# Two largest sorted experts ahead of the four small ones, and the later down weights on ScalarE's DMA queue

## The reference, cut to what matters

```python
DEPTH = 2, SEQ = 512, D_MODEL = 1024, N_EXPERTS = 16, N_GROUPS = 4, TOP_K = 2, D_FF_EXPERT = 256

def reference(...):
    for i in range(DEPTH):
        y = gated_deltanet(x) if i == 0 else latent_attention(x)
        x = layernorm(ALPHA * x + y)
        y = grouped_moe(x, router_w, router_bias, w_gate[i], w_up[i], w_down[i])
        x = layernorm(ALPHA * x + y)

def grouped_moe(x, ...):           # x: 512 tokens
    scores = sigmoid(x @ router_w)
    # one group of four experts is selected per token, and the top two experts in it
    gates = ...                    # (512, 16), two entries per row are not zero
    hid = silu(einsum('td,edf->tef', x, w_gate)) * einsum('td,edf->tef', x, w_up)
    return einsum('tef,efd->td', hid * gates[..., None], w_down)
```

## Time and profile before

| | |
|---|---|
| time, median of 3 runs | 1362.57 us (1362.47 to 1367.99) |
| time of the profiled execution | 1367.03 us |
| its span in the trace | 1365.2 us |
| TensorE busy | 1295.4 us, 95% of the span |
| VectorE, ScalarE, GpSimd busy | 58%, 25%, 22% |
| experts of layer 0, pass 0's first expert matmul to the last pass's end | 734.7 to 881.4 us |
| experts of layer 1, the same | 1182.3 to 1328.9 us |

### The profile page before, as it was taken

How to read it: one execution, slowest core, us unless ns; L and a number is a source line. 1 busy time by engine, 2 the same in 40 slices (tenths; PEclk the granted TensorE clock), 3 DMA queues, 4 the chain that set the end, 5 groups by cost and what they waited for, 6 DMA issues and landing times. The chain is left out here.

```text
span 1365.2 us, 22220 instructions
## 1 busy us (share of the span) xinstructions
PE 1295.4 (95%) x7858; PEld 744.5 (55%) x7858; DVE 791.5 (58%) x1751; ACT 346.4 (25%) x773; POOL 303.2 (22%) x536
## 2 busy tenths in 40 slices
PE   8999999999999999999998998999999998899895
PEld 5467575766758667487754332355454454533232
DVE  2867777676676757675676441294253546644227
ACT  3322322222222222223221221122422322122110
POOL 2264434052340613406022000220000000200025
PEclk9999999999999999999999998999999999899898
DMA  6440505225052250533337999730211138499962
GB/s 213 133 111 19 158 7 164 65 73 157 6 165 65 75 153 13 151 130 89 144 123 282 365 412 411 264 116 1 89 45 38 34 109 319 185 349 411 412 247 107
DMA packets 172631, 218.84 MB, mean 160 GB/s; under 512 B 57297, under 2 KB 107857, under 8 KB 172561
## 3 DMA queue, kind: packets, MB, share of 16 engines
q1 hardware_dynamic: 134736, 167.10, 35.8%
q10 hardware_dynamic: 32736, 32.77, 7.2%
q0 software_dynamic: 5088, 18.02, 3.6%
HBM read 184.58 MB, written 33.29 MB: 160 GB/s over the span
## 5 line engine op out<-in xcount | busy, mean ns | idle before, releaser
L531 PE MATMUL bank<-xT,wgu 128*128 128x512 f32 x448 | 196.2, 593 | 3.0 <-DVE wgu L1236 2.8
L2106 PE MATMUL bank<-wgu,moe_xgT 128*32 128x512 f32 x1120 | 158.8, 606 | 2.9 <-ACT moe_xgT L2224 2.9
L531 PEld LDWEIGHTS bank<-xT,wgu 128*128 128x128 f32 x448 | 83.6, 190 | 100.3 <-issue 100.1
L1236 DVE SCALAR_TENSOR_TENSOR wgu<-bank,taps,wgu 128x510 f32<-128x510 f32 (+1 forms) x128 | 95.6, 748 | 62.6 <-ACT wgu L833 56.7
L617 PE MATMUL bank<-wd,xT 128*128 128x256 f32 x512 | 118.9, 383 | 0.3 <-DVE res L1329 0.3
L583 PE MATMUL bank<-wd,oT 128*128 128x512 f32 x224 | 105.3, 593 | 0.0
L617 PEld LDWEIGHTS bank<-wd,xT 128*128 128x128 f32 x512 | 94.5, 190 | 16.2 <-issue 3.3
L2141 PE MATMUL bank<-wd,moe_hidT 128*32 128x512 f32 x704 | 84.8, 625 | 12.4 <-issue 11.2
L2106 PEld LDWEIGHTS bank<-wgu,moe_xgT 128*32 128x32 f32 x1120 | 43.8, 112 | 73.5 <-issue 65.9
L2406 DVE TENSOR_TENSOR moe_hid<-moe_silu,bank 128x256 f32<-128x256 f32 x22 | 9.3, 421 | 113.0 <-ACT moe_silu L2230 113.0
L2106 PE MATMUL bank<-moe_fifth,moe_xgT 128*32 128x512 f32 x288 | 70.6, 594 | 0.0
(11 more groups left out here) (374 smaller groups left out, 2320.3 us busy)
## 6 DMA issues: line engine op xcount, KB each, us to landing
wd<-moe_w_down SPq DMA_DIRECT2D x32, 1024.0 KB, 13.0
wgu<-moe_w_gate SPq DMA_DIRECT2D x26, 1024.0 KB, 10.5
wgu<-moe_w_up SPq DMA_DIRECT2D x26, 1024.0 KB, 13.4
wgu<-dn_w_in SPq DMA_DIRECT2D x32, 512.0 KB, 4.5
slots_x<-gains SPq DMA_DIRECT2D x5, 1920.0 KB, 10.2
wgu<-gate_rows SPq DMA_DIRECT2D x14, 512.0 KB, 5.3
wd<-dn_w_out ACTq DMA_DIRECT2D x14, 512.0 KB, 4.2
wd<-dn_w_in ACTq DMA_DIRECT2D x7, 1024.0 KB, 5.2
```

The costliest lines, as they stand in the source:

```text
L531: mm = pe.matmul(bank[:], wqkv[:, ct, k], xT[:, k], start=k == 0, stop=k == KD - 1)
L1236: ins = nc.vector.scalar_tensor_tensor(out=conv[:, ct, lo:hi], in0=bank[:, lo + d:hi + d], scalar=w[:, j:j + 1], in1=conv[:, ct, lo:hi], o ...
L2106: mm = pe.matmul(ps[2][seats].rearrange("p (a f) -> p a f", a=2), xgT[:, j % ROW_BUFS, k, seats], gate_up_of(e)[:, :, k], start=k == 0, st ...
```

## The change

It moves the position of the four small experts from v = 5 to 8 to v = 7 to 10 (`FIRST_SMALL` = 7), and puts the two largest sorted experts at v = 5 and 6; the rest keep their order (smallest to larger, the third largest last). With that, which passes a position takes part in is:

| position | 5 | 6 | 7 | 8 | 9 | 10 | 11 to 15 |
|---|---|---|---|---|---|---|---|
| passes before | 3, 4 | 4 | 4, 5 | 5 | 5, 6 | 6, 7 | as after |
| passes after | 3, 4 | 4, 5 | 5 | 5, 6 | 6 | 6, 7 | as before |

So pass 4 needs positions 5, 6, 7 before and 5, 6 after; pass 5 needs 7, 8, 9 before and 6, 7, 8 after; pass 6 needs 9, 10 before and 8, 9, 10 after. What frees a buffer moves too: gate and up 11 wait for pass 5 (before: 4), 13 for pass 6 (before: 5), down 10 for pass 5 (before: 4), down 12 for pass 6 (before: 5); the others keep theirs.

The down matrices of positions 4 to 15 are no longer started by SP but by ScalarE (`next_downs(j)`, behind `results(j)` and ahead of `store(j)`), which reads `order` for each itself. SP starts the gate and up pairs alone, in order of position. The router computes the new places with two more small operations ahead of `place` and one fewer behind it.

```diff
-FIXED, SMALL = 5, 4
+FIXED, SMALL, FIRST_SMALL = 5, 4, 7
-TILES = [v for v in range(NE) for _ in range(2 if FIXED <= v < FIXED + SMALL else 3)]
+TILES = [v for v in range(NE) for _ in range(2 if FIRST_SMALL <= v < FIRST_SMALL + SMALL else 3)]
...
+FIRST_SORTED = TILES.index(FIRST_SMALL) + 3 * (SORTED - 1) - (SORTED - 1)
+WRAP = len(TILES) - TILES.index(FIXED)
...
-            def load_gate_ups(j):
-                for v in range(FIXED, NE):
-                    if LAST_PASS[SLOT_BEFORE[v]] == j:
...
-            def load_downs(j):
-                for v in range(RING, NE):
-                    if LAST_PASS[v - RING] == j:
-                        sp.wait_ge(down_full, j + 1)
-                        sp.dma_start(wd[:, v % RING], pick(d_dram, number[v])).then_inc(d_in[v % RING], 16)
-            load_gate_ups(0)
-            load_downs(0)
-            load_gate_ups(1)
-            for j in range(2, PASSES):
-                if j < FIXED:
-                    load_gate_ups(j)
-                load_downs(j - 1)
-                if j >= FIXED:
-                    load_gate_ups(j)
+            def next_gate_up(v):
+                number = sp.value_load(order[0:1, v - FIXED:v - FIXED + 1], min_val=0, max_val=NE - 1)
+                sp.wait_ge(gu_full, LAST_PASS[SLOT_BEFORE[v]] + 1)
+                sp.dma_start(pair_rows(gate_up_of(v)[:, 0]), pick(g_dram, number)).then_inc(gu_in[SLOT[v]], 16)
+                sp.dma_start(pair_rows(gate_up_of(v)[:, 1]), pick(u_dram, number)).then_inc(gu_in[SLOT[v]], 16)
+            next_gate_up(5)
...
+            next_gate_up(15)
...
+            def next_downs(j):
+                for v in range(RING, NE):
+                    if LAST_PASS[v - RING] == j:
+                        number = v if v < FIXED else act.value_load(order[0:1, v - FIXED:v - FIXED + 1], min_val=0, max_val=NE - 1)
+                        act.wait_ge(down_full, j + 1)
+                        act.dma_start(wd[:, v % RING], pick(d_dram, number)).then_inc(d_in[v % RING], 16)
...
             results(0)
+            act.wait_ge(place_ready, 2)
+            next_downs(0)
             rowsT(1)
             store(0)
...
                 results(j)
+                next_downs(j)
                 store(j)
...
-            nc.vector.tensor_tensor(over[:], rank[:], over_tiles(seats_of[:]), ALU.is_ge)
             step(nc.vector.tensor_reduce(base[:], below[:], AX.X, ALU.add))
+            step(nc.vector.tensor_scalar(key[:], first_tile[:, free], float(len(TILES)), -float(WRAP), ALU.is_ge, ALU.mult))
+            nc.vector.tensor_tensor(first_tile[:, free], first_tile[:, free], key[:], ALU.add)
+            step(nc.vector.tensor_tensor(over[:], rank[:], over_tiles(seats_of[:]), ALU.is_ge))
...
-            step(nc.vector.tensor_scalar(place_of[:], place_of[:], -1.0, float(SORTED - 1), ALU.mult, ALU.add))
-            step(nc.vector.tensor_tensor(more, of_one(number[:, 0:SORTED]), of_other(place_of[:]), ALU.is_equal))
+            step(nc.vector.tensor_tensor(more, of_one(c[:, C_TILE + FIXED:C_TILE + NE]), of_other(first_tile[:, free]), ALU.is_equal))
```

More of the change, by code:

```diff
@@ L47 @@
 C_SUM = C_IOTA + P
-C_ALL = C_SUM + 16
+C_TILE = C_SUM + 16
+C_ALL = C_TILE + 16
 def constants():
@@ L75, in constants @@
     c[:, C_IOTA:C_IOTA + P] = np.arange(P)[None, :]
+    c[:, C_TILE:C_TILE + 16] = [TILES.index(v) for v in range(16)]
     for g in range(4):
@@ L2007, in _ @@
             sp.wait_ge(place_ready, 2)
-            number = {RING: RING}
-            def load_gate_ups(j):
-                for v in range(FIXED, NE):
-                    if LAST_PASS[SLOT_BEFORE[v]] == j:
[L2013 to L2016, removed]
-            def load_downs(j):
-                for v in range(RING, NE):
-                    if LAST_PASS[v - RING] == j:
-                        sp.wait_ge(down_full, j + 1)
-                        sp.dma_start(wd[:, v % RING], pick(d_dram, number[v])).then_inc(d_in[v % RING], 16)
-            load_gate_ups(0)
-            load_downs(0)
-            load_gate_ups(1)
-            for j in range(2, PASSES):
-                if j < FIXED:
-                    load_gate_ups(j)
-                load_downs(j - 1)
-                if j >= FIXED:
-                    load_gate_ups(j)
+            def next_gate_up(v):
[4 more added lines that the diff above has]
+            next_gate_up(5)
+            next_gate_up(6)
+            next_gate_up(7)
+            next_gate_up(8)
+            next_gate_up(9)
+            next_gate_up(10)
+            next_gate_up(11)
+            next_gate_up(12)
+            next_gate_up(13)
+            next_gate_up(14)
+            next_gate_up(15)
             if layer == 0:
@@ L2343, in _ @@
             step(nc.vector.scalar_tensor_tensor(out=extra[:], in0=load[:], scalar=(CAP - 1) / 2.0 - CAP, in1=less_seats[:], op0=ALU.add, op1=ALU.subtract))
-            nc.vector.tensor_scalar(first_tile[:, free], place_of[:], float(SORTED - SMALL - 1), float(len(TILES) - 3 - SORTED + SMALL + 1), ALU.max, ALU.add)
+            nc.vector.tensor_scalar(first_tile[:, free], place_of[:], float(SORTED - SMALL - 1), float(FIRST_SORTED), ALU.max, ALU.add)
             step(nc.vector.tensor_scalar(extra[:], extra[:], 1.0 / CAP, WHOLE, ALU.mult, ALU.add))
```

## The result

| | before | change |
|---|---|---|
| median | 1363.8 us (1360.81 to 1369.34, 20 runs) | 1367.61 us (1361.98 to 1372.29, 20 runs) |
| profiled execution, span | | 1369.43 us, 1367.6 us |

The ratio is 1.0028, 95% interval 1.0017 to 1.0039: 3.8 us slower by the medians. The forecast was 1.1 us faster.

What follows compares the result with a forecast made beforehand. TensorE and full DMA engines limit closely together; what counts is which weight lands last before which pass. Per layer 8.9 us added, 9.5 (9.4) removed: -1.1 us for both, 1361.5 us from the 1362.57 median, range 1353 to 1370.

Steps and rivals of the forecast that it cites:

- what the change adds: Per layer, two new waits in pass 6, slower clock behind them and router operations: 8.9 us in sum.
- the first wait: Pass 6's gate_up idles 3.6 us (low end 1.0) for up 10, since down 8 is moved ahead of it.
- the second wait: Pass 6's down waits 2.1 us (up to 4.1, or none) for down 10 on ScalarE's queue.
- the router: Two dependent small operations ahead of place, each about 0.2 us: 0.4 us a layer, hidden by nothing.
- What the change removes: Waits for weights, mainly in pass 5, and the slower clock behind them: 9.5 and 9.4 us, 18.9 in all.
- The clock: Slower matmuls after pass 6's idle times: 2.0 us (1.7 to 2.7) behind gate_up's, 0.8 behind down's, counted half.
- At nothing: Costed zero: ScalarE's reads and issues (some 2.5 us a pass), later rows and stores, later weights from pass 7 on.
- B: Rival: both pass 6 waits small, up 10 only 1.0 us late, down 10 in time: 1346.5 us; chance 0.20.
- C: Rival: down 10 lands later than taken, at 14.1 us a wait of 7.0 us: 1375 us; chance 0.12.

Runs made afterwards that it cites:

- e10: Kernel before with only the change's 16 more constant columns (64 bytes per partition), unused: ratio 1.0026, 1369.40 against 1365.09 us.
- the padded change: The whole change with 112 further unused constant columns, table 512 bytes longer than before: ratio 0.9985 to the kernel before, 1360.24 against 1362.62 us.
- c1: The kernel before, unchanged, executed once more for a second profile: 1364.33 us.
- e3: The change, but only 1/16 of down 8 is loaded: ratio 0.9977 to the kernel before, 1360.52 against 1363.72 us.
- e8: The change with down 8 whole, back on SP's queue behind gate and up 10: ratio 1.0037 to the kernel before, 1368.75 against 1363.52 us.
- e9: The change with down 9 issued one pass later: ratio 1.0060 to the kernel before, 1374.79 against 1365.09 us.
- e11: Kernel before with the change's constants and its two more router operations ahead of place (factor zero): ratio 1.0037, 1369.07 us.
- e15: The change's order, down 10 alone on ScalarE's queue, table padded to 512 bytes longer: ratio 0.9929 to the kernel before, 1353.55 against 1362.62 us.
- e4: Kernel before's order and router, change's constants, down 9 alone on ScalarE, down 8 ahead of gate and up 11: ratio 0.9984, 1361.47 against 1363.72 us.
- e6: The change's order and router, down 10 alone on ScalarE, other down matrices on SP: ratio 0.9982 to the kernel before, 1362.15 against 1363.8 us.
- e12: Kernel before, constants unchanged, down 9 alone on ScalarE, SP's list reordered (gate and up 12 ahead of down 10): ratio 0.9936, 1356.63 against 1365.09 us.
- e1: The change's order of positions and router, but all down matrices back on SP: ratio 1.0005 to the kernel before, 1364.88 against 1363.72 us.

## Why the prediction was off

**The step that failed: the list of what the change adds.** It had the first wait, the second wait and the router, and lacked the constants table. `C_TILE` stood in the code that I read and I costed it as nothing, without a word. It is worth +3.5 us in e10 (0.26% of 1365) and turns the sign: the padded change measures 0.9985, 2.0 us faster (the interval just reaches no change), and the forecast for the work that I did cost was 1.1 us faster. In the sum itself the term that is off is the first wait with its clock, 15.9 us for both layers instead of 11.2. By the ratios the shift makes 0.43% of the change (1.0028 against 0.9985), 5.9 us, give or take 3 us by the two intervals.

**What the change removes** held in kind. No wait over 0.5 us is left in pass 5, and its `down` is back at 3.64 us. The size came from one execution: 18.9 us in that, 17.2 in c1. With 17.2 the same sum would have come to 0.6 us slower, so that the forecast had a sign at all is owed to which execution was profiled.

**First wait**: right place, right load, right cause (e3, e8), 5.02 and 6.57 us instead of 3.6. Up 10 landed 69.4 us after the row loads were issued, against 65.7 before, so 3.7 later where I took 2.6. In the padded change up 10 lands after 64.7 and 66.0 us, the wait is 2.59 and 2.55, and no slower matmuls follow it. So without the shift the term would have been large enough, as far as one execution shows. By its rate alone (402 for 412 GB/s, 2.4%) the shift would make the loads of these 65 us some 1.6 us later, and the change and its repeat are 1.2 to 5.6 later than the padded change; what makes the rest is open. Whether down 8 costs up 10 more than its bytes (2.6 us) I can't tell: e3 and e8 give 2.7 to 6.3. That e9 moves it so little speaks against down 9 as a large part of it.

**Second wait**: forecast 1.1 + 9.2 - 8.2 = 2.1, measured 2.37 and 1.12. Down 10 took 9.8 us in layer 0 and 8.5 in layer 1 from issue to landing, on both sides of the 9.2 that I took, and was issued 0.8 us after the `down` instead of 1.1: the read of `order` takes 0.28 us, not the 0.8 of the earlier trace rows. The trace of before had the right row, since SP reads the same words there in 0.26 to 0.30 us.

ScalarE's reads in the change:

```profile
L2246 ACTq TENSOR_LOAD <-moe_order x22: 279/284/302, 775.8 to 1306.1; - x22
```

**The clock**: after 2.37 us of idle the `down` took 5.34 instead of 3.64 us in layer 0, after 1.12 us it did not in layer 1. Counting half of 1.7 was right on the average of the two. Behind the first wait I took 2.0, and it is 1.7 in layer 0 and 2.6 in layer 1.

**The router**: 0.41 us by the trace, as forecast. The timed pair e10 and e11 is level, which neither bears out nor refutes a term of 0.8 us.

**At nothing**: ScalarE's reads and issues cost nothing that shows, and pass 7 and later of the change do not wait. In the padded change, whose passes run ahead, pass 8's `gate_up` waits 0.79 and 2.14 us: behind each wait that is cured stands the next, and part of what pass 6 gets back goes there. So that the padded change comes close to the forecast is in part luck: in its trace the two waits of pass 6 make 7.5 us for both layers where the forecast had 17.0 with the clock, and pass 8 adds 2.9 that it had at nothing.

**The rivals.** *B* (the waits small) did not come: the first wait shrinks to B's 1.0 us only in e15 (0.25 and 0.77), where down 8 stays behind up 10. *C* (down 10 late by its 14 us) is refuted by 9.8 and 8.5 us. The rule of the Trainium skill that was set beside it (DMA: Bandwidth & Descriptors, Rules for kernel authors: spreading transfers over the engines that issue them doesn't help bandwidth) agrees with the rates: the padded change moves 412 GB/s with the later down matrices on ScalarE's queue, the kernel before 412 with all on SP's. It doesn't speak of when one load lands, and there the queue counts: 9.7 and 8.8 us for down 9 in e4 instead of 14.1, both 1 MB (the prediction's 8.7 against 17.4 us set 512 KB beside 1 MB). At an equal rate it matters which load stands behind which. The result lay inside the forecast's range, for a reason that was not in it.

## What to carry to other kernels

Cost the rows of a diff that only allocate: before trusting a small difference, compare the DMA rate of the same stretch in both traces, and try the new kernel with the table padded, here to 512 bytes more (one edit). Where the DMA engines were full, a second queue made no room; it let loads past others. Here it paid to give it the one that was late and nothing else. And read the waits that a forecast removes from more than one execution.

## What the runs showed of the hardware

- A table of constants longer by 64 bytes per partition, ahead of the other buffers: the full DMA engines moved 401 to 403 GB/s in the change, its repeat and e10, instead of 412 to 413; by 128 bytes, 404 and 405; by 512 bytes, 412 and 413. Which buffer's or tensor's address matters, which shifts between 128 and 512 bytes are harmless, and by what mechanism, was not taken apart.
- Down 9 or down 10, 1 MB, landed 8.2 to 9.8 us after its issue on ScalarE's queue (change, its repeat, e4, e6, e12, e15), while up 10 on SP's queue took 15.9 to 23.9 in the same kernels.
- Waits of 2.4 to 2.9 us were followed by slower matmuls in some executions and not in others, about 1.7 us each: 2.37 us in the change was and 2.40 in its repeat was not, 2.91 in layer 1 of e1 was and in layer 0 was not.
